# Scan of a two-block kernel: causal mask as a product with the scores, exponents bounded on VectorE, one exponential a pair

## What is computed

```python
def step(state, inp):
    x_c, a_c, B_c, C_c = inp
    cum = jnp.cumsum(a_c, axis=1)
    cum_t = jnp.moveaxis(cum, 1, -1)
    seg = cum_t[..., :, None] - cum_t[..., None, :]
    decay = jnp.exp(jnp.where(causal, seg, -jnp.inf))
    cb = jnp.einsum('bign,bjgn->bgij', C_c, B_c)
    y_intra = jnp.einsum('bgij,bghij,bjghp->bighp', cb, decay, x_c)
    y_inter = jnp.einsum('bign,bghpn->bighp', C_c, state) * jnp.exp(cum)[..., None]
    ...
    return new_state, y_intra + y_inter
```

## Time and profile before

| | |
|---|---|
| median of three runs | 1594.31 us |
| profiled execution, its own time | 1593.19 us |
| its span in the trace | 1591.5 us |
| busy: TensorE, VectorE, ScalarE, GpSimd | 98%, 62%, 49%, 11% of the span |
| stretch of the scan | 238.8 us (first L982) to 366.5 us (last L999) |
| granted clock of TensorE in the scan | 1.00 |
| chain that ended last | TensorE 92%, VectorE 5%, ScalarE 2% |

### The profile page before, as it was taken

The page is one execution under the profiler, slowest core; times in us unless marked ns, Lnnn a source line. Parts: engine busy times, 40 slices in busy tenths (PEclk is TensorE's granted clock), DMA queues, the critical chain, the costliest instruction groups (busy, mean ns, idle before and its releaser), DMA issues.

```text
span 1591.5 us, 30332 instructions
## 1 busy us (share of the span) xinstructions
PE 1557.3 (98%) x12594; PEld 1513.0 (95%) x12594; DVE 989.7 (62%) x1277; ACT 774.4 (49%) x1021; POOL 173.3 (11%) x137
## 2 busy tenths in 40 slices
PE   8999999989999999999999999999999999999997
PEld 4999998879999999999999899999999999899997
DVE  5898995345766555555475775555655558765545
ACT  4555555555455434544443654443544435554433
POOL 0300003333100010000022020001300013020001
PEclk9999999999999999999999999999999999999999
DMA  7976763324555554555535335555455553455550
GB/s 303 379 290 217 285 229 120 107 82 158 186 186 184 186 186 152 193 184 184 186 135 204 134 117 194 184 184 186 148 185 184 185 187 130 159 185 184 184 185 28
DMA packets 42186, 289.67 MB, mean 182 GB/s; under 512 B 4876, under 2 KB 7052, under 8 KB 7533
## 3 DMA queue, kind: packets, MB, share of 16 engines
q1 hardware_dynamic: 41244, 284.44, 49.6%
q0 software_dynamic: 848, 3.88, 0.6%
HBM read 285.15 MB, written 3.15 MB: 181 GB/s over the span
## 4 chain that ended last, share of the span: by engine, by line
PE 92%; DVE 5%; ACT 2%; issue 1%; DMA 1%; SPq 0%; ACTq 0%; DVEq 0%
PE banks L628 22%; PE banks L631 22%; PE banks L630 22%; PE banks L733 6%; PE banks L736 6%; PE banks L735 6%; DVE w_lo L1643 1%; DVE XS L1791 1%; PE banks L982 1%; PE banks L998 1%; PE banks L764 1%; PE banks L984 0%; DMA raw<-in_panels 0%; ACT w_hi L1186 0%; DVE H L1799 0%
## 5 line engine op out<-in xcount | busy, mean ns | idle before, releaser
L1643 DVE TENSOR_TENSOR w_lo<-raw,w_hi 128x1024 fp32r<-128x1024 f32 x490 | 614.9, 1263 | 478.9 <-ACT w_hi L1186 473.6
L1186 ACT ACTIVATE w_hi<-raw 128x1024 fp32r<-128x1024 f32 x490 | 515.6, 1057 | 566.8 <-PE banks L631 409.5
L628 PE MATMUL banks<-H,w_lo 128*128 128x256 f32 x1920 | 542.0, 282 | 3.2 <-DVE H L1799 1.6
L630 PE MATMUL banks<-H,w_hi 128*128 128x256 f32 x1920 | 540.3, 281 | 0.0
L631 PE MATMUL banks<-H,w_hi 128*128 128x256 f32 x1920 | 540.2, 281 | 0.0
L628 PEld LDWEIGHTS banks<-H,w_lo 128*128 128x128 f32 x1920 | 361.3, 188 | 6.5 <-issue 3.4
L630 PEld LDWEIGHTS banks<-H,w_hi 128*128 128x128 f32 x1920 | 361.4, 188 | 0.0
L631 PEld LDWEIGHTS banks<-H,w_hi 128*128 128x128 f32 x1920 | 361.4, 188 | 0.0
L628 PE MATMUL banks<-HH,w_lo 128*128 128x256 f32 x960 | 270.1, 281 | 0.0
L630 PE MATMUL banks<-HH,w_hi 128*128 128x256 f32 x960 | 270.1, 281 | 0.0
L631 PE MATMUL banks<-HH,w_hi 128*128 128x256 f32 x960 | 270.1, 281 | 0.0
(11 more groups left out here) (290 smaller groups left out, 1644.7 us busy)
## 6 DMA issues: line engine op xcount, KB each, us to landing
raw<-in_panels SPq DMA_DIRECT2D x269, 1024.0 KB, 4.8
bias_rows<-rev POOLq DMA_DIRECT2D x1, 2048.0 KB, 15.2
XS<-in_x_t SPq DMA_DIRECT2D x1, 1024.0 KB, 6.8
near<-bias_rows POOLq DMA_DIRECT2D x8, 128.0 KB, 3.4
out_t<-XS SPq DMA_DIRECT2D x4, 256.0 KB, 2.6
ws<-in_ws_t POOLq DMA_DIRECT2D x1, 512.0 KB, 8.3
cols<-in_cols SPq DMA_DIRECT2D x1, 180.0 KB, 2.5
wdt<-in_wdt POOLq DMA_DIRECT2D x1, 128.0 KB, 4.9
```

Source lines behind the costliest of these rows:

```text
L628: pe.matmul(acc, w_lo[:, panel_slot, at:at + P], operand[:, kk, 0, :], start=starts and c == chunks[0], stop=False)
L630: pe.matmul(acc, w_hi[:, panel_slot, at:at + P], operand[:, kk, 1, :], start=False, stop=False)
L1186: act.activation(w_hi[:, sl, w], raw[:, r, w], ACT.Copy).then_inc(panel_hi, 1)
L1643: vec.tensor_tensor(w_lo[:, sl, w], raw[:, r, w], w_hi[:, sl, w], ALU.subtract).then_inc(panel_lo, 1)
```

## The change

The mask no longer enters as -1e30 on the exponents. Instead the scores are multiplied by a tile `causal` of zeros and ones, and every exponent is bounded by zero before the exponential, so that what the mask cancels stays finite. Allowed exponents are never above zero.

- TensorE: the mask matmuls go; `cum_r` is laid out as three blocks of 128 tokens (the last block twice), so a head takes one matmul of 384 columns. The running sums for it are made with 256 columns in place of 128.
- VectorE: `exponents(n)` adds the bias to the rows in PSUM and takes the minimum with zero, four instructions a pair, into `decay(n)`; `scores_masked(g)` multiplies the scores with `causal` in place of ScalarE's copy; `decayed_scores(n)` makes the product that GpSimd made.
- ScalarE: one exponential of 128x768 a pair, in place in `decay(n)`.
- GpSimd: only gating and `y_lo` stay in the scan.
- `decay_rows(n)` now waits for the exponents of pair n-1, not for its exponentials.

```diff
@@ -248,4 +248,5 @@
         ea = sb("ea", [P, 32], F32, phase)
-        cum_r = sb("cum_r", [64, T], F32R, phase)
+        cum_r = sb("cum_r", [64, 3 * P], F32R, phase)
         pick_r = sb("pick_r", [64, 32], F32R, phase)
+        causal = sb("causal", [P, 3, P], F32, phase)
         phase.close()
@@ -564,7 +565,2 @@
                     gating(n - 2)
-                pool.wait_ge(S["exp_done"], 4 * (n + 1))
-                pool.wait_ge(S["cb_copied"], n // 2 + 1)
-                two = decay(n).rearrange("p (r i) -> p r i", r=2)
-                pool.tensor_tensor(two, two, cb[:, n // 2 % 2, :].unsqueeze(1).to_broadcast([P, 2, 3 * P]),
-                                   ALU.mult).then_inc(S["m_done"], 1)
                 if n >= 12:
@@ -903,4 +899,6 @@
                     pe.matmul(banks[rows, 6, 0:P], a_v[:, 0, :], tri[:, :], start=True, stop=True)
-                    pe.matmul(banks[rows, 6, P:T], a_v[:, 0, :], ones[:, :], start=True, stop=False)
-                    last = pe.matmul(banks[rows, 6, P:T], a_v[:, 1, :], tri[:, :], start=False, stop=True)
+                    second = banks[rows, 6, P:3 * P].rearrange("q (a i) -> q a i", a=2)
+                    pe.matmul(second, a_v[:, 0, :], ones[:, :].unsqueeze(1).to_broadcast([P, 2, P]), start=True, stop=False)
+                    last = pe.matmul(second, a_v[:, 1, :], tri[:, :].unsqueeze(1).to_broadcast([P, 2, P]),
+                                     start=False, stop=True)
                 last.then_inc(S["cum_done"], 1)
@@ -975,12 +973,6 @@
                     if n:
-                        pe.wait_ge(S["exp_done"], 4 * (n - 1) + 2 * (r + 1))
+                        pe.wait_ge(S["exponents"], 4 * (n - 1) + 2 * (r + 1))
                     h = 2 * n + r
                     pick = pick_r[:, h:h + 1].to_broadcast([64, P])
-                    for at, tokens in ((0, slice(0, T)), (T, slice(P, T))):
-                        to = banks[:, 5 + r, at:at + tokens.stop - tokens.start]
-
-                        pe.matmul(to, pick, cum_r[:, tokens], start=at == 0, stop=False)
-                    diagonal = banks[:, 5 + r, :].rearrange("p (a i) -> p a i", i=P)[:, 0:3:2, :]
-                    last = pe.matmul(diagonal, ident_r[:, :], never[:, :].unsqueeze(1).to_broadcast([P, 2, P]),
-                                     start=False, stop=True)
+                    last = pe.matmul(banks[:, 5 + r, 0:3 * P], pick, cum_r[:, :], start=True, stop=True)
                 last.then_inc(S["row_done"], 1)
@@ -1385,3 +1377,3 @@
                     act.wait_ge(S["cum_done"], 1)
-                    act.activation(cum_r[:, :], banks[0:64, 6, 0:T], ACT.Copy).then_inc(S["cum_hi"], 1)
+                    act.activation(cum_r[:, :], banks[0:64, 6, 0:3 * P], ACT.Copy).then_inc(S["cum_hi"], 1)
                 for half in range(2):
@@ -1417,19 +1409,5 @@
 
-            def cb_copy(g):
-                act.wait_ge(S["cb_done"], g + 1)
-                if g >= 2:
-                    act.wait_ge(S["m_done"], 2 * (g - 1))
-                act.activation(cb[:, g % 2, :], banks[:, 3, 0:3 * P], ACT.Copy).then_inc(S["cb_copied"], 1)
-
             def decays(n):
-                act.wait_ge(S["row_done"], n + 1)
-                if n >= 2:
-                    act.wait_ge(S["y_done"], n - 1)
-                for r in range(2):
-                    h = 2 * n + r
-                    for t, (at, size) in enumerate(((0, T), (T, P))):
-
-                        act.activation(decay(n)[:, 3 * P * r + at:3 * P * r + at + size],
-                                       banks[:, 5 + r, at:at + size], ACT.Exp,
-                                       bias=dtv[:, 4, t, h:h + 1]).then_inc(S["exp_done"], 1)
+                act.wait_ge(S["exponents"], 4 * (n + 1))
+                act.activation(decay(n), decay(n), ACT.Exp).then_inc(S["exp_done"], 1)
 
@@ -1459,4 +1437,2 @@
                 decays(n)
-                if n % 2 == 0:
-                    cb_copy(n // 2)
                 if n >= 2:
@@ -1891,2 +1867,4 @@
             vec.tensor_scalar(never[:, :], tri[:, :], -1.0, -MASKED, ALU.add, ALU.mult).then_inc(S["never_set"], 1)
+            vec.memset(causal[:, 1, :], 1.0)
+            vec.tensor_copy(causal[:, 0:3:2, :], tri[:, :].unsqueeze(1).to_broadcast([P, 2, P])).then_inc(S["causal_set"], 1)
             vec.tensor_tensor(pick_r[:, :], ident[0:64, 0:32], ident[0:64, 32:64], ALU.add).then_inc(S["pick_set"], 1)
@@ -1935,3 +1913,3 @@
                 vec.wait_ge(S["cum_hi"], 1)
-                vec.tensor_tensor(cum_r[32:64, :], banks[32:64, 6, 0:T], cum_r[32:64, :], ALU.subtract)\
+                vec.tensor_tensor(cum_r[32:64, :], banks[32:64, 6, 0:3 * P], cum_r[32:64, :], ALU.subtract)\
                     .then_inc(S["cum_lo"], 1)
@@ -2012,2 +1990,11 @@
 
+            def scores_masked(g):
+                vec.wait_ge(S["cb_done"], g + 1)
+                if g == 0:
+                    vec.wait_ge(S["causal_set"], 1)
+                if g >= 2:
+                    vec.wait_ge(S["m_done"], 2 * (g - 1))
+                vec.tensor_tensor(cb[:, g % 2, :], banks[:, 3, 0:3 * P], causal[:, :, :].rearrange("p a i -> p (a i)"),
+                                  ALU.mult).then_inc(S["cb_copied"], 1)
+
             def tokens_times_dt(g):
@@ -2028,2 +2015,22 @@
 
+            def exponents(n):
+
+                vec.wait_ge(S["row_done"], n + 1)
+                if n == 1:
+                    vec.wait_ge(S["silu_done"], SSM_GROUPS)
+                if n >= 2:
+                    vec.wait_ge(S["y_done"], n - 1)
+                for r in range(2):
+                    h = 2 * n + r
+                    for t, (at, size) in enumerate(((0, T), (T, P))):
+                        vec.tensor_scalar(decay(n)[:, 3 * P * r + at:3 * P * r + at + size], banks[:, 5 + r, at:at + size],
+                                          dtv[:, 4, t, h:h + 1], 0.0, ALU.add, ALU.min).then_inc(S["exponents"], 1)
+
+            def decayed_scores(n):
+                vec.wait_ge(S["exp_done"], n + 1)
+                vec.wait_ge(S["cb_copied"], n // 2 + 1)
+                two = decay(n).rearrange("p (r i) -> p r i", r=2)
+                vec.tensor_tensor(two, two, cb[:, n // 2 % 2, :].unsqueeze(1).to_broadcast([P, 2, 3 * P]),
+                                  ALU.mult).then_inc(S["m_done"], 1)
+
             def y_variance(g):
@@ -2078,3 +2085,5 @@
                 if n % 2 == 0:
+                    scores_masked(n // 2)
                     tokens_times_dt(n // 2)
+                exponents(n)
                 if n == PAIRS - 1:
@@ -2088,2 +2097,3 @@
                             gate_times(g, h)
+                decayed_scores(n)
                 if 11 <= n < 15:
```

More of the change, by code:

```diff
@@ L303, in two_blocks @@
             "wdt_hi wdt_lo dt_raw dt_y dt_exp dt_one dt_ln dt_ea dt_a pick_set bs_clear bs_rounded bs_split y_log cum_done cum_got cum_hi cum_lo "
-            "cb_done cb_copied xt_done xdt_done row_done exp_done never_set m_done y_done y_skip "
+            "cb_done cb_copied exponents causal_set xt_done xdt_done row_done exp_done never_set m_done y_done y_skip "
             "y_gated y_sq y_sums y_var y_root y_f y_hi y_lo "
```

## The result

| | before | changed |
|---|---|---|
| median of the runs, us | 1594.31 | 1619.62 (1618.13 to 1619.78) |
| ratio, 95% interval | | 1.0155 (1.0143 to 1.0167) |
| span of the profiled execution, us | 1591.5 | 1618.0 |
| mean granted clock | 0.995 | 0.989 |

What follows compares the result with a forecast made beforehand. The order of the queues, not busy shares, was taken to decide; along TensorE 0.9 + 2.5 + 4.0 + 2.8 + 1.9 + 3.0 = 15.1 us on the profiled 1593.19, with the median 1.1 above, gave 1609.4, range 1602 to 1619.

Steps and rivals of the forecast that it cites:

- running sums: Ahead of the scan: eight passes at 256 columns take 0.11 us more each on TensorE, +0.9.
- opening, to the first group sums: Scan's start: exponents, exponential and product follow one another, so the first group sums start at 269.0, not 266.8: +2.2 us.
- to the cycle's zero: Scores behind the first group sums, up to the next head products: a wait of 1.0 with 0.63 saved, +0.3 us.
- three cycles: Three plain cycles of two pairs, 276.8 to 322.0 us: each ends at 16.3 against 14.94, +4.0 us in all.
- roots' cycle: Cycle where ScalarE's four roots already hold back the group sums and VectorE's normalising steps the scores: 0.
- the next one: Cycle behind the roots, where TensorE already waits: 1.9 us ahead of group sums, 0.9 for the product ahead of scores, +2.8.
- chain a once more, and the end: Longer path through exponents, exponential and square to the last group sums, +1.9 us; wait ahead of the last head products, +3.0.
- TensorE would not take the saving: Rejected the rival that the new waits stay hidden and TensorE wins 10.1 less 0.9 us: 1585, 7%.
- both chains: Plain cycle: product, exponents, exponential, square delay group sums (wait 1.7 us); w_hi, w_lo, product, variance delay scores (1.0): +1.33 a cycle.
- the clock: Rival: TensorE falls to half clock behind pauses ahead of the first group sums and at the end, +2.6 us each: 1613, 12%.
- The rival of steps that don't overlap: Each VectorE step costs its whole duration, about +5 us: 1614.5, 6%.

Runs made afterwards that it cites:

- three moves in the queues: Changed kernel with the product ahead of w_lo, the square ahead of the exponential, variance and normalising steps ahead of the odd pair's product: 1586.37 us, ratio 0.9955.
- the late idle matmuls: Changed kernel with matmuls that compute nothing ahead of TensorE's waits from the fourth group on and the last head products only: 1615.70 us, ratio 1.0135.
- the first run with idle matmuls: Changed kernel with matmuls that compute nothing ahead of all long waits of TensorE, opening included: 1617.71 us, ratio 1.0136.

## Where the prediction was right, and where it failed

The span's 26.5 us against the forecast's 15.1, stretch by stretch of TensorE:

| stretch | forecast | measured |
|---|---|---|
| running sums | 0.9 | 0.4 |
| opening, to the first group sums | 2.2 | 5.7 |
| to the cycle's zero | 0.3 | 0.4 |
| three cycles | 4.0 | 5.6 |
| roots' cycle | 0 | 1.8 |
| the next one | 2.8 | 4.4 |
| chain a once more, and the end | 4.9 | 8.1 |

**Right:** that TensorE would not take the saving; both chains, step by step; a wait of 1.7 (1.81) ahead of the group sums and of 1.0 (1.00) ahead of the scores; exponential 0.84, product 0.95, the overlap of VectorE's neighbours (w_lo of 1.22 with the product 1.14 behind its start). The experiments confirm the cause in the plain cycle: with nothing taken off VectorE, three moves in the queues bring it from 16.67 to 13.6, TensorE's own.

**Wrong, the late cycles and the end (6.6 us short).** The step that failed most is the clock, put outside the sum: "The engine was lightly used before that pause and wouldn't be here", at 12%. A TensorE that had been busy throughout fell to half clock four times from 346.2 us on, and the late idle matmuls, which kept it up, show that this cost 5.1 us. Taken off, it leaves 1614.5, inside the range. With the clock up, the cycle behind the roots' comes to +2.8, as forecast; the roots' cycle comes to +1.0 where 0 was put, and the end to +5.5 for 4.9. That rest of 1.5 is part price: two products take 2.02 and 2.05 beside GpSimd's y_lo, 1.1 over the price each, in chains that end in a wait. I had priced the product by rows in which GpSimd rested.

The 12% stood against a row of the trace that showed a wait of 3.08 and a fall behind it. The reading of that row was also short: its window of 5 us cuts off a stretch that lasts from 25.3 to 32.1 us. And 2.6 each makes 1612.0 for one fall and 1614.6 for two, not 1611 to 1613.5.

**Wrong, the opening (3.5 us short).** The clock fell here too, but that cost next to nothing, as the first run with idle matmuls shows. The chain itself was too short. When each of its steps was done:

| step | forecast | measured |
|---|---|---|
| start of the first exponential | 247.4 | 249.1 |
| first product | 252.3 | 254.2 |
| third pair's exponents | 259.9 | 262.2 |
| w_hi behind the gate's eviction | 264.1 | 267.8 |
| square | 269.0 | 272.8 |

Of each difference 0.3 is the later start of the scan. Two steps were mistaken. "ScalarE's table load ends at 247.4" left the load where it stood; but it belongs to the first exponential, and it ran only when that one's new wait, for VectorE's exponents, was over, so its 1.28 came on top. And w_hi was put right behind the gate's eviction, where it waited 1.35 for TensorE to release its half panel, because TensorE's filler had itself waited for that eviction:

```profile
247.82 1.28 ACT L1412 ACT_TABLE_LOAD   x1 [1.43 <-DVE ev L2026]
...
266.69 1.06 ACT L1178 ACTIVATE w_hi<-raw 128x1024 fp32r<-128x1024 f32 x1 [1.35 <-PE banks L732]
```

The remaining 0.8 or so is the price of the exponents, three times. So the first long wait, 2.97, stood ahead of the first head products, where the forecast had none. This is read from the trace; no run moved the table load ahead of that wait, and all the versions carry it.

**Mis-sized, the exponents.** Four take 1.38 or 1.39, not 1.17, and the masked scores 0.56, not 0.46; the scaling is as priced. The exponents make 0.2 on chain a and the same again on b by way of w_hi; the cycle of 16.67 is 0.37 above 16.3, over three cycles 1.1 of the 1.6 missing there.

**Mis-sized without effect:** the rows, 0.54 a pair where 0.65 was forecast (saved rows vanish in waits), and the running sums, whose columns of the two row groups ran partly beside one another.

The rival of steps that don't overlap (1614.5) is nearer in time, and is refuted: product to skip is 0.87 for 0.95. The Trainium skill (VectorE: DVE Perf Modes, "The DRAIN you can't avoid") has the next step wait for the pipe to empty, but adds that one which isn't held starts earlier, and that half is what these rows show.

A rule that I had not weighed agrees with the runs. In this case the steps with two sources in SBUF slow down beside GpSimd (w_lo from 1.22 to 2.0 beside its product, product from 0.95 to 2.05 beside y_lo), while the exponents, with a source in PSUM, stay at 476 ns beside its gating. The kernel before had it too: w_lo takes 2.45 at 253.6 us, beside GpSimd's product. The Trainium skill (SBUF — State Buffer, "SBUF: two separate sides") says that such a VectorE step and a GpSimd step that reads SBUF take one port pair in turn, the first to start keeping it to its end.

Open: which waits bring a fall of the clock, since like waits did and didn't; and what share of the 5.1 us each late fall has.

## What to carry to other kernels

Before work is moved to an engine with room, write the timetable of one cycle with the slack ahead of each step of the bounding engine; where the slack is under a microsecond, the place of the new step in its queue decides the sign, and moving it is the cheap remedy. A forecast wait of 3 us on TensorE should carry the half clock behind it, at its full price where TensorE bounds what follows and at nothing where it would wait again. When an instruction gets a new wait, ask what else moves behind that wait, such as a table load. Compare a reordered version with the old kernel reordered likewise. Price an instruction by a row with the same kinds of operands, and with the same neighbours on the engines beside it.

## What the runs showed of the hardware

- A scan in which TensorE was busy until then: half clock behind a wait of 2.97 us, for 7 us, and again during or within 1.4 us behind waits of 1.99, 2.87, 3.75 and 3.79 us, but not behind one of 3.49. Idle matmuls ahead of the waits kept the clock up late (1.00 for 0.89), and in the opening they only moved the fall.
- ScalarE's table load (1.28 us) started 0.1 us behind the last exponent that its exponential waits for, not ahead of the wait, though ScalarE had been idle for 1.43 us.
- VectorE's w_lo takes 1.22 us, and 2.0 beside a GpSimd product of 1.8 that started 0.9 earlier.
- A tensor_scalar from PSUM of 256 columns: 413 ns with constants, 475 with an operand by partition, with one operation or two.
- A matmul of 64 rows and 384 columns: 0.28 us until the next of its kind, 0.26 until the filler's, 0.37 until the mask matmul, the same as two of 256 and 128 ahead of the mask.
